# Second-layer dilated attention on one Trainium2 core: keys of the second and third pattern read in place

## The reference, cut to what matters

```python
B_SLOTS = 8
B_PATTERNS = ((128, 1), (512, 4), (2048, 16))

def to_sub(x, r):
    n, t = x.shape[:2]
    rest = x.shape[2:]
    x = jnp.swapaxes(x.reshape((n, t // r, r) + rest), 1, 2)
    return x.reshape((n * r, t // r) + rest)

def dilated_prompt(q, k, v, slopes):
    n = q.shape[0]
    outs, lses = [], []
    for gi, (w, r) in enumerate(B_PATTERNS):
        qs = to_sub(q[:, :, gi], r)[:, :, :, None]
        o, lse = banded_attention(qs, to_sub(k, r), to_sub(v, r), slopes[gi][:, None], r, w // r)
        outs.append(from_sub(o[:, :, :, 0], n, r))
        lses.append(from_sub(lse[..., 0], n, r))
    return combine_groups(outs, lses)
```

## Time and profile before

| what | value |
|---|---|
| median of 3 runs | 2654.59 us (2653.87 to 2658.92) |
| the profiled execution's own time | 2653.27 us |
| its span, first to last instruction | 2651.4 us |
| mean granted TensorE clock | 0.976 |
| PE busy | 2512.3 us, 95% |
| DVE, ACT, POOL busy | 38%, 25%, 17% |
| prompt attention of layer 2 (first score to last value product) | about 1495.6 to 1660.3 us |
| sample attention of layer 2 | about 1661 to 1768 us |

### The profile page before, as it was taken

The page is one execution under the profiler, slowest core; times in us unless marked ns, Lnnn a source line. Parts: engine busy times, 40 slices in busy tenths (PEclk is TensorE's granted clock), DMA queues, the critical chain, the costliest instruction groups (busy, mean ns, idle before and its releaser), DMA issues. The chain is left out here.

```text
span 2651.4 us, 42321 instructions
## 1 busy us (share of the span) xinstructions
PE 2512.3 (95%) x16458; PEld 2431.9 (92%) x16458; DVE 999.1 (38%) x1979; ACT 659.4 (25%) x1253; POOL 439.0 (17%) x458
## 2 busy tenths in 40 slices
PE   6988799999999999999999999788999999999996
PEld 6877599999999999999999899468999999999995
DVE  5344534332322232336212366436332232332335
ACT  3344423220111111113100267224320111111112
POOL 2243201100110200101111333331101100101100
PEclk9999899999999999999999999899999999999998
DMA  3011113113113113111211233843113113113111
GB/s 151 28 43 33 60 59 122 48 40 110 48 36 105 49 39 111 48 33 47 89 66 40 88 89 110 296 168 111 46 36 116 40 42 108 48 34 116 42 36 77
DMA packets 65121, 199.23 MB, mean 75 GB/s; under 512 B 7640, under 2 KB 11096, under 8 KB 64248
## 3 DMA queue, kind: packets, MB, share of 16 engines
q1 hardware_dynamic: 64120, 193.17, 22.0%
q0 software_dynamic: 912, 4.85, 0.5%
HBM read 182.21 MB, written 51.05 MB: 88 GB/s over the span
## 5 line engine op out<-in xcount | busy, mean ns | idle before, releaser
L1398 PE MATMUL PS<-XH,WH 128*128 128x384 f32 (+1 forms) x2880 | 637.1, 331 | 32.1 <-DVE XL L931 28.8
L904 DVE TENSOR_TENSOR WL<-RAW,WH 128x1024 fp32r<-128x1024 f32 (+3 forms) x200 | 223.3, 1118 | 1176.9 <-ACT WH L612 1176.3
L1398 PE MATMUL PS<-XH,WL 128*128 128x384 f32 (+1 forms) x2784 | 617.0, 329 | 0.0
L1398 PE MATMUL PS<-XL,WH 128*128 128x384 f32 (+1 forms) x2688 | 596.0, 330 | 0.0
L1398 PEld LDWEIGHTS PS<-XH,WH 128*128 128x128 f32 x2880 | 496.4, 190 | 34.6 <-issue 28.0
L457 POOL TENSOR_TENSOR RAW<-RAW,GAIN 128x1024 f32<-128x1024 f32 x114 | 221.3, 1944 | 1686.9 <-DMA RAW<-in_w_gu 1405.3
L612 ACT CAST WH<-RAW 128x1024 fp32r<-128x1024 f32 (+3 forms) x200 | 189.0, 947 | 1197.5 <-PE PS L1398 1167.3
L1398 PEld LDWEIGHTS PS<-XH,WL 128*128 128x128 f32 x2784 | 479.1, 189 | 0.0
L1398 PEld LDWEIGHTS PS<-XL,WH 128*128 128x128 f32 x2688 | 462.4, 189 | 0.0
L1398 PE MATMUL PS<-HL,WH 128*128 128x384 f32 (+1 forms) x1056 | 231.8, 327 | 0.0
L1398 PE MATMUL PS<-HH,WL 128*128 128x384 f32 (+1 forms) x1056 | 231.8, 327 | 0.0
(11 more groups left out here) (183 smaller groups left out, 2474.3 us busy)
## 6 DMA issues: line engine op xcount, KB each, us to landing
RAW<-in_w_gu SPq DMA_DIRECT2D x88, 512.0 KB, 3.5
out_bkS<-in_bk_in SPq DMA_DIRECT2D x8, 2032.0 KB
out_bvS<-in_bv_in SPq DMA_DIRECT2D x8, 2032.0 KB
RAW<-in_w_dn SPq DMA_DIRECT2D x32, 384.0 KB, 3.0
KC<-in_bk_in SPq DMA_DIRECT2D x8, 1536.0 KB, 9.7
VC<-in_bv_in SPq DMA_DIRECT2D x8, 1536.0 KB, 7.2
RAW<-in_w_dn SPq DMA_DIRECT2D x32, 320.0 KB, 2.9
XT<-in_xT SPq DMA_DIRECT2D x16, 544.0 KB, 5.1
```

Of the source, the lines that this page charges most:

```text
L904: nc.vector.tensor_tensor(lo[:, j, 0:nk * P], RAW[:, j, 0:nk * P], hi[:, j, 0:nk * P].bitcast(F32), ALU.subtract).then_inc(S["wl"], 1)
L1398: ins = mm(PS[:, 3 * j + c, 0:width], w[:, j, k * P:(k + 1) * P], x(k, a, width), start=(k == 0 and n == 0), stop=(k == nk - 1 and n == 2))
```

## The change

KP4, KP16, the semaphore `kperm`, `reorder` and its 8 POOL copies are gone, and so is PE's wait. For groups 1 and 2 `keys_b` gives PE a strided view of KB: 128 or 256 elements 4 elements (16 bytes) apart in group 1, and two runs of 64 elements 16 elements (64 bytes) apart in group 2. The values are fetched as before. In the freed room VC[1] becomes a buffer of its own (VC1); PSB moves to the room of KB, PTS and OM move a little. SP issues VC1, TSB and TSW right after the values of group 2, ahead of the stores of group 1. VC[0] and both KC stay where they were.

```diff
--- before.py
+++ after.py
@@ -170,20 +170,19 @@
         WH2 = at("WH2", [P, 2, KT * P], R + 18432, F32R)
         WL2 = at("WL2", [P, 2, KT * P], R + 26624, F32R)
         VG = [at("VG0", [P, 8, 512], o_xh), at("VG1", [P, 8, 512], o_xh + 16384)]
-        KP = [at("KP4", [P, 4 * SEQ], o_xl), at("KP16", [P, 4 * SEQ], o_xl + 16384)]
         TAB = [at("TAB1", [P, 8, 256], o_raw), at("TAB4", [P, 8, 256], R), at("TAB16", [P, 8, P], R + 8192)]
 
         UST = [at("UST0", [P, UROW], o_xh + 32768), at("UST1", [P, UROW], o_xl + 32768)]
 
         KC = at("KC", [P, 2, 4, KEPT], R + 12288)
-        VC = at("VC", [P, 2, 6, 512], R + 36864)
+        VC = [at("VC0", [P, 6, 512], R + 36864), at("VC1", [P, 6, 512], o_xl + 7584)]
         SQN = at("SQN", [P, NG, 4, 32], o_xl)
         TSB = at("TSB", [P, R16 + R4 + R1], o_xl + 1536)
         TSN = at("TSN", [P, NG, NEW], R + 79872)
         TSW = at("TSW", [P, NG, 120], o_xl + 6144)
-        PSB = at("PSB", [P, 2, SCOLS], o_xl + 7584)
-        PTS = at("PTS", [P, 7, P], o_xl + 18336)
-        OM = at("OM", [P, 512], o_xl + 21920)
+        PSB = at("PSB", [P, 2, SCOLS], R + 49152)
+        PTS = at("PTS", [P, 7, P], o_xl + 19872)
+        OM = at("OM", [P, 512], o_xl + 23456)
         OS = at("OS", [P, P], o_xl + 34400)
         MG = [at("MG0", [P, NG, UROW], o_xl + 27296), at("MG1", [P, NG, UROW], R)]
         PS = ctx.enter_context(nc.psum_tensor("PS", [P, 8, 512], F32))
@@ -192,7 +191,7 @@
             sq sqs sums std rb eps xh xn silu gt yg yp yt yout scaled hh hx
             qev a_free a_score a_ttr a_exp a_rl a_norm a_tr a_pev0 a_pev1 a_pv a_out ohi olo xre
             stage clear score ttr exp tr pev0 pev1 pv stat onorm0 onorm1
-            tabA nsink tab1 tab4 tab16 kperm vnew vst_out vg0 vg1 ust0 ust1
+            tabA nsink tab1 tab4 tab16 vnew vst_out vg0 vg1 ust0 ust1
             cA tsa sa_q sa_s sa_ttr sa_exp sa_es sa_p sa_tr sa_evA sa_evD sa_pv sa_out sa_outlo
             kc0 kc1 vc0 vc1 tsb sb_tab sb_stage sb_zero sb_s sb_ttr sb_exp sb_p sb_tr sb_evA sb_evD sb_pv sb_os sb_otr sb_oh sb_ol
             turn mg0 mg1 m_min m_d m_w m_sum m_c m_add m_om m_tr m_hi m_lo rows_out copies""".split()
@@ -380,20 +379,20 @@
             v16 = vrow[0:SEQ].rearrange("(i n r) d -> r i n d", r=2, n=8)
             for r in range(2):
                 sp.dma_start(VG[0][64 * r:64 * r + 64, :, :], v16[r]).then_inc(S["vg0"], 16)
+            sp.dma_start(VC[1][:], values_of(1)).then_inc(S["vc1"], 16)
+            sp.dma_start(TSB[:], t["tabSB"]).then_inc(S["tsb"], 16)
+            sp.dma_start(TSW[:], t["tabSW"]).then_inc(S["tsb"], 16)
             store_u(sp, 4, t["u"][1].rearrange("(h p b) d -> b h p d", h=2, b=4), 1)
 
             sp.wait_ge(S["stage"], 64)
             sp.wait_ge(S["score"], 64)
             sp.wait_ge(S["rows_out"], 80)
             sp.dma_start(KC[:, 0], keys_of(0)).then_inc(S["kc0"], 16)
-            sp.dma_start(VC[:, 1], values_of(1)).then_inc(S["vc1"], 16)
-            sp.dma_start(TSB[:], t["tabSB"]).then_inc(S["tsb"], 16)
-            sp.dma_start(TSW[:], t["tabSW"]).then_inc(S["tsb"], 16)
             u2 = t["u"][2].rearrange("(i b h r) d -> b h r i d", r=2, h=2, b=4)
             store_u(sp, 8, u2, 2, 0, 3)
             sp.wait_ge(S["stage"], 96)
             sp.dma_start(KC[:, 1], keys_of(1)).then_inc(S["kc1"], 16)
-            sp.dma_start(VC[:, 0], values_of(0)).then_inc(S["vc0"], 16)
+            sp.dma_start(VC[0][:], values_of(0)).then_inc(S["vc0"], 16)
             store_u(sp, 8, u2, 2, 3, 4)
             sp.wait_ge(S["score"], 96)
             sp.wait_ge(S["ttr"], 96)
@@ -412,7 +411,7 @@
                     sp.wait_ge(S["sb_s"], b - 1)
                     sp.dma_start(KC[:, j], keys_of(b)).then_inc(S[f"kc{j}"], 16)
                     sp.wait_ge(S["sb_pv"], b - 1)
-                    sp.dma_start(VC[:, j], values_of(b)).then_inc(S[f"vc{j}"], 16)
+                    sp.dma_start(VC[j][:], values_of(b)).then_inc(S[f"vc{j}"], 16)
                     sp.wait_ge(S["m_om"], b - 1)
                     merge_load(b, j)
             loop(sp, 1, 4, sample_loads)
@@ -522,23 +521,12 @@
                     pool.wait_ge(S["score"], 32 * g + 8 * i + u - 7)
                     stage(QB[:, ds((4 * g + u % 4) * SEQ + (2 * i + u // 4) * P, P)], u)
 
-            def reorder(p, x):
-
-                r = PATTERNS[1 + x][1]
-                nc.gpsimd.tensor_copy(KP[x][:, ds(p * SEQ, SEQ)].rearrange("p (r i) -> p r i", r=r),
-                                      KB[:, ds(p * SEQ, SEQ)].rearrange("p (i r) -> p r i", r=r)).then_inc(S["kperm"], 1)
-
             def stage_keys(i, first=False):
 
                 for u in range(8):
                     if not first:
                         pool.wait_ge(S["score"], 8 * i + u - 7)
                     stage(QB[:, ds((u % 4) * SEQ + (2 * i + u // 4) * P, P)], u)
-                    if u % 4 == 3:
-                        x = u // 4
-                        pool.wait_ge(S["stage"], 8 * i + u + 1)
-                        reorder(i, x)
-                        pool.wait_ge(S["kperm"], 2 * i + x + 1)
             pool.wait_ge(S["slab"], PLAN.end("qB"))
             stage_keys(0, True)
             loop(pool, 1, 4, stage_keys)
@@ -1687,17 +1675,12 @@
 
 
             def keys_b(g):
-                src = KB if g == 0 else KP[g - 1]
-
                 def keys(i, u, w, first):
                     p, h = u % 4, u // 4
                     if g == 0:
-                        off = 0 if first and h == 0 else (2 * i - 1 + h) * P
-                    elif g == 1:
-                        off = 2 * i * P
-                    else:
-                        off = (2 * i + h) * P
-                    return src[:, ds(p * SEQ + off, w)]
+                        return KB[:, ds(p * SEQ + (0 if first and h == 0 else (2 * i - 1 + h) * P), w)]
+                    by = KB[:, p * SEQ:(p + 1) * SEQ].rearrange("p (n r) -> p r n", r=PATTERNS[g][1])
+                    return by[:, ds(i, 1), 0:w] if g == 1 else by[:, ds(2 * (2 * i + h), 2), :]
                 return keys
 
             def values_b(g):
@@ -1713,8 +1696,6 @@
                     return VG[g % 2][:, ds(m, 1), d:d + HD].rearrange("p m d -> p (m d)")
                 return values
             for g in range(NG):
-                if g:
-                    pe.wait_ge(S["kperm"], 8)
                 attention(32 * g, 4, int(g == 0), widths_b(g), keys_b(g), values_b(g), None,
                           lambda: pe.wait_ge(S[f"vg{g % 2}"], (16, 64, 48)[g]))
 
@@ -1776,7 +1757,7 @@
                         o = PS[32 * p:32 * p + 32, 7, 0:P]
                         f = slice(p * P, (p + 1) * P)
                         if c < 6:
-                            mm(o, PTS[:, c, 32 * p:32 * p + 32], VC[:, j, c, f], start=(c == 0), stop=False)
+                            mm(o, PTS[:, c, 32 * p:32 * p + 32], VC[j][:, c, f], start=(c == 0), stop=False)
                         else:
                             ins = mm(o, PTS[0:NEW, 6, 32 * p:32 * p + 32], VNB[0:NEW, f], start=False, stop=True)
                 ins.then_inc(S["sb_pv"], 1)
```

## The result

| what | before | after |
|---|---|---|
| median of 4 runs each, taken side by side | 2656.76 us (2653.87 to 2659.62) | 2686.66 us (2681.21 to 2689.03) |
| ratio after to before, 95% interval | | 1.011 [1.0089, 1.013] |
| the profiled execution's own time | 2653.27 us | 2686.99 us |
| its span | 2651.4 us | 2685.2 us |
| mean granted TensorE clock | 0.976 | 0.976 |

The change makes the kernel 29.9 us slower by the medians, 24 to 35 us by the interval. The forecast was 2688, in a range of 2653 to 2695.

What follows compares the result with a forecast made beforehand. The prediction took PE to bound the kernel, with POOL's copies hidden. Copies -0.5, stride +34.5 and moved loads 0 gave +34.0 us on 2654.6, so 2688 us, in a range of 2653 to 2695.

Steps and rivals of the forecast that it cites:

- What bounds the kernel: All three groups of the prompt attention are bound by PE, busy 95% of the span; POOL's work is hidden except 0.5 us.
- Part 1, the copies: POOL's 8 copies of keys, 16 us of work, go; only PE's 0.5 us of waiting in group 0 is gained.
- Part 2, the stride: PE's 40960 strided key columns in groups 1 and 2 go from 0.82 to 1.70 ns: 36.0 us, 34.5 after idle time.
- 1.5 of idle time: PE's idle time in group 2, at most 1.5 us, which could absorb some of the stride's cost.
- The reason for 1.70: DVE's strided reads cost 1.70 ns an element, taken as what the memory needs by itself, so PE would pay it too.
- both passes read by themselves: Rival: a score record streams keys twice, each pass paying 1.70 ns, 3.40 a column: 106 us more, 2759 us; chance 0.06.
- The hidden case: Rival: PE's 0.82 ns a column hides the stride, under about 0.95 ns: 2654 us, not slower; chance 0.33.
- The factor: Rival: a stride multiplies PE's 0.82 ns by DVE's 1.61 to 1.70: 20 to 24 us more, about 2676; chance 0.09.
- Part 3, the moved loads: VC1, TSB and TSW ahead of group 1's stores delay the first store by 7.6 us, which nobody waits for: 0 us.
- The 1.6 us of cover: In group 1, the margin between the first store's latest landing, 1587.7, and DVE's need of UST0 at 1589.34.
- The wait that stays: In the sample part, DVE's 6.02 us wait for MG, with PE's value products 4.30 us late, should remain.
- The sum: Whole kernel: -0.5 for copies, +34.5 for the stride, 0 for moved loads, +34.0 us in all.

Runs made afterwards that it cites:

- e4: Changed kernel with POOL's 8 copies of keys put back, read by nobody, and SP waiting for them before the early loads: 2689.7 us, ratio to before 1.0114.
- e10: Kernel before, with DVE's projected queries of groups 1 and 2 reading only one operand strided, first SBUF's, then PSUM's: 2652.21 us, one run.
- e3: Changed kernel with staged queries and KB rounded to float32r, so a score product is one record in place of two: 2646.77 us, one run.
- e9: Changed kernel with float32r scores and keys read at stride 2 in group 1 and stride 3 in group 2: 2648.19 us, one run.
- e2: Changed kernel with float32 keys read at stride 2 in group 1 and stride 3 in group 2: 2665.26 us, one run.
- e5: Changed kernel with VC1, TSB and TSW issued where they were before, behind KC[0] and group 1's stores: 2688.01 us, ratio to before 1.0112.
- b1: Kernel before, with VC[0]'s load moved behind MG's first: 2654.1 us against 2658.02, ratio 0.9984.

## Why the forecast held, and where its reason didn't

- **What bounds the kernel.** Right. PE's score records grew and the groups grew with them, while POOL's 15.6 us less bought about 1 us.
- **Part 1, the copies: -0.5 us.** The size was low: group 0 shows -1.5 us in the profiled pair and 1.0 us in e4. The rows of PE's waits counted only the 0.5 us that loads waited visibly, and 0.3 of those stay in the changed kernel, without any copy:

```profile
PEld PS L1457 <- POOL STG L474: 0.3, 1, 0.3
```

- **Part 2, the stride: +34.5 us.** It measured +31.0. Per column 1.76 ns (stride 4) and 1.66 (stride 16) stood against the 1.70 that I took. Group 1: 16 narrow units by 0.43 and 16 wide ones by 0.91 are 21.4 us; the stage shows 21.0, the forecast said 22. In group 2 the forecast had 14.4 us less 1.5 of idle time, 12.9, and the stage shows 10.0. Two terms of that were mis-sized. The 32 narrow units cost 0.40 us each, 12.8 us in all: that is 0.78 ns for each of their columns, where the forecast had 0.88. And the idle time that took up the rest was 2.8 us, not at most 1.5. I had read it from PE's busy share in one window of 40 us, which can't show all of it, since the printed duration of a record runs on while the next one waits. In the kernel before, 8 of the 28 units behind the first four of group 2 have their transposes 0.54 to 0.92 us behind their scores in place of 0.50, 1.9 us together. The latest belongs to the score at 1639.72 of the earlier trace rows:

```profile
1640.64 0.41 PE L1480 MATMUL PS<-IDN,SB 128*128 128x128 f32 x2 [0.25 <-ACT PT L740]
```

  In the changed kernel none of the 28 is over 0.90. Counted by whole units, 40.6 - 32 x 1.11 = 5.1 us of the group were slack before, and 50.6 - 32 x 1.53 = 1.6 after.
- **The reason for 1.70.** This step failed, though its number held. It said that 1.70 ns is what the memory needs for an element by itself, so that PE would meet the same floor as DVE. e10 confirms that DVE's 1.7 to 1.8 ns come from its operand in SBUF. e3 shows that PE gets a strided key in 0.9 ns. That a float32 record pays twice that lands on DVE's figure, and nothing here says why the two agree: as far as the runs show, the price was right by luck. The rival "both passes read by themselves" fits strides of 4 and more with 2 x 0.88 ns in place of its 2 x 1.70, and fails at stride 2 (e9). What a strided float32 column costs is measured; what it is made of stays open.
- **The hidden case, at 0.33.** It was to decide below 0.95 ns a column. It is true of stride 2, at 0.86 (e2), and false from stride 3 on. The Trainium skill, "TensorE: Matmul & The Clock Gate", section "What happens when you issue a matmul", calls throughput purely the number of columns: the trace agrees at strides 1 and 2 of float32 and disagrees at 3 and above, with 1.31 to 1.76 ns against 0.82. In float32r it disagrees at stride 2 already, with 0.51 us for two wide records against 0.32.
- **The factor, at 0.09.** DVE's factor of 1.6 to 1.7 is not PE's, which is 2.0 to 2.1; PE starts from a faster pace.
- **Part 3, the moved loads: 0.** Right by e5. The first store was held up by 2.3 us, where I had allowed 7.6. The 1.6 us of cover that I had counted were not put to the test, since in the longer group 1 they became 12.4.
- **The wait that stays.** It stayed: 5.7 us at its longest. That it costs something, 4 us by the medians, is shown by b1.
- **The sum.** -0.5 + 34.5 = 34.0 forecast, 29.9 by the medians, 29.5 by the three groups. The 33.8 us between the two profiled spans looks closer, but 5.9 of it come from ahead of the change and are spread.

## What to carry to other kernels

A permuted copy on an engine with room is cheap as long as PE covers it (here 1 us for eight), and it is paid once; a strided moving operand is paid by PE with each product that reads it. With float32 a stride of 2 was nearly free here, and one of 4 or more doubled the time of a column. Before one trades a copy for an access pattern, see which engine is full, and count the columns that read it. For the slack of a stage, take its length less its units by their usual pace: a busy share leaves out what hides in the printed durations.

## What the runs showed of the hardware that I had not expected

- PE's pace for a float32 record by stride of the moving operand: 0.82, 0.86, 1.31, 1.76, 1.66 ns a column at 1, 2, 3, 4 and 16. In float32r, 0.90 at 2 and at 4 alike. That fits no single size of line for both types.
- A stride in PSUM costs DVE nothing (548 and 552 ns against 550), the same stride in SBUF 53% (839).
- Faster products can come with a lower clock. With float32r scores the clock fell behind a pause of 0.8 us at the start of group 2 and then stood at 0.50 of full, though PE was busy for 40.00 of 40 us; the unchanged transposes and value products then took nearly twice as long, and the kernel as a whole gained nothing (ratio 0.9996).
